# A two-block transformer kernel on one core: score banks, the place of a head's last mix, five more orders, and who splits one weight tile

## The chip, the cores and the metric

The kernel is one launch on one core of a Trainium2 chip. The metric is the device time in microseconds. TensorE (PE in the rows) multiplies; VectorE (DVE), ScalarE (ACT) and GpSimd (POOL) compute beside it; SyncE (SP) issues most loads. The granted clock is the share of TensorE's full clock of 2.4 GHz that it was given; 0.50 is its lower level, 1.2 GHz.

## The reference

All in float32, for 512 tokens of width 1024 and a context of 256 tokens.

```python
def reference(x, p, ...):
    x = first_block(x, p, ...)        # NSA and sliding-window attention, conv MLP, gate
    return second_block(x, c_2, ctx_2, ...)

def second_block(x, c, ctx, ...):     # layer 0: diff_attention_mixer, layer 1: gqa_mixer
    h  = rms_norm(x, pre_g[i]) * (1.0 + scale) + shift
    hc = rms_norm(xc, pre_g[i]) * (1.0 + cscale) + cshift
    # diff attention, 8 heads: keys and values of tokens and context together
    o1 = sweep_attention(q[..., 0, :], k[..., 0, :], v)
    o2 = sweep_attention(q[..., 1, :], k[..., 1, :], v)
    o = rms_norm(o1 - lam * o2, subln_g) * (1.0 - lam_init)
    y = (o * silu(z)) @ w_out
    x = x + gate * rms_norm(y, post_g[i])   # layer 0 also for the context
    # layer 1: rms_norm of q and k by head, rope, softmax attention, 2 key heads
```

## The kernel before

Each engine has its own instruction list, written out by hand, and semaphores ("signals") join them: `x.up(event)` counts, `wait_ge(x.at(event))` waits. The order of an engine's instructions is the order of its code, so an instruction that waits holds up all behind it.

**Products.** Float32 is kept by splitting each operand into a high and a low half: `three` (L482) issues three matmuls per chunk (L483 to L485): high by high and the two mixed products. Weights are loaded by SyncE in pairs of 128-row chunks into two raw buffers (`sp_program`, L371; a buffer is loaded again when its pair is split) and split by GpSimd (`pool_program`, L432: L470 makes the high half `w_hi`, L472 the low half `w_lo`, twice per pair). The tile ("kv", 1) is the second of all; then GpSimd zeroes keys.

**End of the first attention (project_out).** For each of four row tiles t: product with w_o, norm, addition; ScalarE squares (L1513) and scales the row (L1517), TensorE turns it (`turn_out`, L517), ScalarE writes h_hi (L1495), VectorE h_lo (L2311). `pe_first_cols` (L934) multiplies the first 256 tokens by the next weight in four units of eight chunks (24 matmuls) between the last turns.

**Gate stage.** Units u = 0 to 7 on VectorE; in u = 7 the sum of the last mod piece (`dve_mod_sum`, `dve_mod_end`, L2553), which TensorE turns at L894.

**Heads.** Eight heads of the difference attention. A head has six query tiles, `HEAD_TILES` = context tiles 4 and 5, then token tiles 0 to 3; n = 0 to 11 counts a tile's two halves. For each n: scores on TensorE (L1184; a context tile has 256 columns in bank 0, a token tile 2 × 384 in banks 0 and 1), the minimum on VectorE (L2797), the exponential with its sum on ScalarE (L2034). After both halves VectorE mixes them (`dve_head_mix`, L2805, L2807, L2809), TensorE turns the mix in two parts through one bank (L1200), ScalarE copies each part (L2045), and two tiles later come the values (L1214). The last tile's mix is done in the next head at n = 0, behind that head's first minimum. Between the scores TensorE works off, by `HEAD_FILL`, the chunks of the next head's projections ("beside": 4 chunks behind n = 0, 2 and 1 behind n = 1); their rows go through ScalarE (L1972, L1979, L1980) and VectorE (ropes L2743 to L2752, L2769, L2770) and TensorE (L1133).

**out0 and the last layer.** `pe_out0` multiplies by w_out and turns rows 0 to 5 (ScalarE: tmp L1505, h_hi L1509; VectorE: h_lo L2318), then the key rows kv8. `dve_keys8` (L2892) finds the roots of two key tiles (L2271 to L2287), scales by them (L2903) and ropes them; `dve_grouped` (L2985) begins with the query tables gq, q_cos, q_sin, L2990 to L2996; `dve_turned8` (L2919) gives k_lo, and TensorE turns keys at L1333.

## Time and profile before

| | us |
|---|---|
| median of 3 runs | 1715.09 (1714.62 to 1715.71) |
| the profiled execution, its own time | 1713.1 |
| its span | 1711.8 |
| its granted clock, mean | 0.966 |
| TensorE matmul busy | 1576.5 (92%) |
| VectorE busy | 1043.0 (61%) |
| GpSimd busy | 708.9 (41%) |
| ScalarE busy | 623.5 (36%) |
| TensorE's waits for L2034 before L1184, from 928 to 1290 us, 13 of them | 19.5 |

The time of a run is some 1.3 us longer than the span of the trace. A matmul's duration in a row overlaps the next one's; their starts show the pace. A number in square brackets at the end of a timeline row is the time for which the engine did nothing before it, and the arrow names the instruction whose end released it.

### The profile page before, as it was taken

Reading aid. Unit: us, or ns where it says so; the run is one execution under the profiler, and the core shown is the slowest. Engines: PE = TensorE matmul, PEld = TensorE weight load, DVE = VectorE, ACT = ScalarE, POOL = GpSimd, SP = SyncE. Lnnn points to the kernel's source line nnn. Section 1 sums busy time; section 2 is a strip of 40 time slices with the busy share of each in tenths; the row PEclk is TensorE's granted clock in tenths of the full one; section 3 lists DMA queues with packets and bytes.
Section 4 is the critical chain, followed back from the end, with each engine's and each line's share of the span. In section 5 each row is a group of like instructions: output and inputs, shape, how many; then the busy total and the mean of one; then the engine's idle time right before and its main releaser. Section 6 shows DMA issues by size and latency. Waiting matters only on the chain.

```text
span 1711.8 us, 21954 instructions
## 1 busy us (share of the span) xinstructions
PE 1576.5 (92%) x7933; PEld 1305.5 (76%) x7933; DVE 1043.0 (61%) x2136; ACT 623.5 (36%) x1506; POOL 708.9 (41%) x676
## 2 busy tenths in 40 slices
PE   5998799989999999999899999999997988899997
PEld 4786344788877887877788988898895777788886
DVE  7636665447777658658555665565566366665644
ACT  3213566231222210123633443444344356344431
POOL 6855000346776749667313303312334213333430
PEclk9997999989999999999999999999999999999999
DMA  6622000424444445553211001101112321110221
GB/s 181 196 72 87 1 1 1 136 82 141 131 125 133 135 157 178 175 168 123 84 28 50 27 24 50 50 13 38 50 38 62 133 77 50 50 50 25 74 87 50
DMA packets 115884, 142.58 MB, mean 83 GB/s; under 512 B 11048, under 2 KB 75200, under 8 KB 115776
## 3 DMA queue, kind: packets, MB, share of 16 engines
q1 hardware_dynamic: 89968, 91.77, 17.6%
q10 hardware_dynamic: 25808, 49.40, 8.9%
q8 instruction: 64, 1.05, 0.2%
q14 instruction: 44, 0.36, 0.1%
HBM read 132.74 MB, written 8.40 MB: 82 GB/s over the span
## 4 chain that ended last, share of the span: by engine, by line
PE 35%; DVE 9%; ACT 4%; issue 2%; ACTq 0%; DVEq 0%
PE ps L483 7%; PE ps L484 7%; PE ps L485 7%; PE ps L1214 3%; PE ps L1184 3%; PE ps L1407 2%; PE ps L1384 2%; PE ps L1200 2%; PE ps L1133 1%; PE ps L1396 1%; ACT tmp L1505 1%; DVE st L2797 1%; DVE newton L2281 1%; ACT p L2034 1%; DVE p L2809 1%
## 5 line engine op out<-in xcount | busy, mean ns | idle before, releaser
L470 POOL TENSOR_SCALAR w_hi<-w_raw 128x512 fp32r<-128x512 f32 x316 | 238.6, 755 | 718.7 <-PE ps L485 552.8
L472 POOL TENSOR_TENSOR w_lo<-w_raw,w_hi 128x512 fp32r<-128x512 f32 x316 | 438.6, 1388 | 26.4
L483 PE MATMUL ps<-w_hi,h_hi 128*128 128x384 f32 (+2 forms) x768 | 283.4, 369 | 3.0 <-DVE h_lo L2861 1.0
L484 PE MATMUL ps<-w_lo,h_hi 128*128 128x384 f32 (+2 forms) x768 | 269.1, 350 | 0.0
L485 PE MATMUL ps<-w_hi,h_lo 128*128 128x384 f32 (+2 forms) x768 | 268.6, 350 | 0.0
L483 PE MATMUL ps<-h_hi,w_hi 128*128 128x512 f32 (+1 forms) x616 | 245.9, 399 | 8.0 <-POOL w_lo L472 4.1
L484 PE MATMUL ps<-h_lo,w_hi 128*128 128x512 f32 (+1 forms) x616 | 238.5, 387 | 0.0
L485 PE MATMUL ps<-h_hi,w_lo 128*128 128x512 f32 (+1 forms) x616 | 238.4, 387 | 0.0
L2531 DVE SCALAR_TENSOR_TENSOR mod_acc<-mod_piece,csil,mod_acc 128x512 f32<-128x512 f32 x140 | 157.7, 1166 | 25.6 <-DMA mod_piece<-in_ada_w 21.2
L483 PEld LDWEIGHTS ps<-w_hi,h_hi 128*128 128x128 f32 x768 | 148.6, 194 | 14.6 <-issue 1.6
L484 PEld LDWEIGHTS ps<-w_lo,h_hi 128*128 128x128 f32 x768 | 148.6, 193 | 9.6 <-issue 0.5
L485 PEld LDWEIGHTS ps<-w_hi,h_lo 128*128 128x128 f32 x768 | 147.9, 193 | 10.3
L483 PEld LDWEIGHTS ps<-h_hi,w_hi 128*128 128x128 f32 x616 | 117.5, 191 | 32.1 <-POOL w_lo L472 5.0
L485 PEld LDWEIGHTS ps<-h_hi,w_lo 128*128 128x128 f32 x616 | 117.2, 190 | 25.8
L484 PEld LDWEIGHTS ps<-h_lo,w_hi 128*128 128x128 f32 x616 | 117.8, 191 | 22.3
L2034 ACT ACTIVATE p<-ps,st 128x768 f32<-128x768 f32 (+1 forms) x96 | 72.9, 759 | 114.6 <-DVE st L2797 114.6
L2797 DVE TENSOR_REDUCE st<-ps 128x1 f32<-128x768 f32 (+1 forms) x96 | 74.4, 775 | 64.3 <-PE ps L1184 64.3
L483 PE MATMUL ps<-w_hi,g_hi 128*128 128x512 f32 x240 | 98.0, 408 | 4.9 <-POOL w_lo L472 4.7
L485 PE MATMUL ps<-w_hi,g_lo 128*128 128x512 f32 x240 | 95.8, 399 | 0.0
L484 PE MATMUL ps<-w_lo,g_hi 128*128 128x512 f32 x240 | 95.8, 399 | 0.0
L2045 ACT COPY p_turned<-ps 128x512 f32<-128x512 f32 (+1 forms) x80 | 36.6, 457 | 115.5 <-PE ps L1200 115.4
L2769 DVE SCALAR_TENSOR_TENSOR q<-ps,q 64x256 fp32r<-64x256 f32 x48 | 20.5, 428 | 93.6 <-ACT k_hi L1980 93.1
(322 smaller groups left out, 2840.1 us busy)
## 6 DMA issues: line engine op xcount, KB each, us to landing
...
w_raw<-in_a_w_in SPq DMA_DIRECT2D x128, 128.0 KB, 2.3
w_raw<-in_w_down SPq DMA_DIRECT2D x22, 512.0 KB, 3.9
w_raw<-in_b_w_in SPq DMA_DIRECT2D x20, 512.0 KB, 3.7
w_raw<-in_w_out SPq DMA_DIRECT2D x16, 512.0 KB, 3.8
w_raw<-in_w_in SPq DMA_DIRECT2D x8, 512.0 KB, 4.0
w_raw<-in_w_o SPq DMA_DIRECT2D x8, 512.0 KB, 3.8
```

Source lines behind the costliest of these rows:

```text
L470: pool.tensor_scalar(hi[:, e, :], raw[:, e, :], 1.0, 0.0, ALU.mult, ALU.add).then_inc(*s["pool_step"].up())
L472: m = pool.tensor_tensor(lo[:, e, :], raw[:, e, :], hi[:, e, :], ALU.subtract)
L483: pe.matmul(out, a[0], b[0], start=start, stop=False)
L484: pe.matmul(out, a[0], b[1], start=False, stop=False)
L485: return pe.matmul(out, a[1], b[0], start=False, stop=stop)
L1184: m = pe.matmul(k.ps[:, j, 0:cols], k.q6[:, b, sub, t * P:(t + 1) * P], kk[:, b, sub, k0 + j * cols:k0 + (j + 1) * cols], start=first, sto ...
L1200: m = pe.transpose(k.ps[:, 4, a * P:(a + 1) * P], k.p6[:, i % 2, c0:c0 + P], k.ident[:, :])
L1214: m = pe.matmul(out, k.v6[:, hd % 2, c, :], k.at6[:, c, :], start=c == chunks[0], stop=c == TA - 1)
L2034: act.activation(folded(k.p6[:, i % 2 if sub == 0 else 2, 0:w], bs), bank_view(k, bs, P, cols), ACT.Exp, bias=f[:, sub:sub + 1], scale=-1. ...
L2045: act.copy(k.at6[:, chunks[0]:chunks[-1] + 1, (t % 2) * P:(t % 2 + 1) * P], k.ps[:, 4, 0:P * len(chunks)].rearrange("p (c n) -> p c n", n= ...
L2531: m = dve.scalar_tensor_tensor(acc, piece, w, acc, ALU.mult, ALU.add)
L2797: dve.tensor_reduce(k.st6[:, i % 4, sub:sub + 1], bank_view(k, bs, P, cols), AX.XY if len(bs) == 2 else AX.X, ALU.min).then_inc(*s["head_l ...
```

## The change

Seven places; what each does:

- Tile ("kv", 1): ScalarE writes the high halves, one activation of 128x1024 per pair, behind its early loads and ahead of its copies of the key halves; GpSimd writes only the low halves and waits for ScalarE's signal.
- project_out: TensorE turns row 2 behind the unit i = 1 (was 2) and row 3 behind six chunks of the unit i = 3 (was behind the whole); ScalarE squares row 3 before the h_hi of row 2 (was behind).
- Gate stage: the last mod piece's sum and end move on VectorE from u = 7 to u = 6, before a turn.
- Heads: context scores alternate between banks 0 and 1, and wait for the exponential two before, where the bank was last read.
- Heads: the last tile's mix stands behind its own head's last minimum (n = 11), not in the next head.
- out0: TensorE turns row 0 behind both halves of tile 3.
- out0 on VectorE: the query tables are made at t = 4 of the loop; the roots of the first keys stand before the last turn, with no wait for the table load.

```diff
@@ -416,6 +416,10 @@
+BY_SCALAR = ("kv", 1)
 def pool_zero_keys(k, pool):
@@ -465,10 +469,13 @@
                     pool.wait_ge(*s["roped8"].at(("kv8", TX + 1)))
+            if tile == BY_SCALAR:
+                pool.wait_ge(*s["act_step"].at(("w_hi", q)))
             for e in range(2):
-                pool.tensor_scalar(hi[:, e, :], raw[:, e, :], 1.0, 0.0, ALU.mult, ALU.add).then_inc(*s["pool_step"].up())
-                pool.wait_ge(*s["pool_step"].now())
+                if tile != BY_SCALAR:
+                    pool.tensor_scalar(hi[:, e, :], raw[:, e, :], 1.0, 0.0, ALU.mult, ALU.add).then_inc(*s["pool_step"].up())
+                    pool.wait_ge(*s["pool_step"].now())
                 m = pool.tensor_tensor(lo[:, e, :], raw[:, e, :], hi[:, e, :], ALU.subtract)
@@ -598,6 +605,20 @@
     return None
+def score_banks(n):
+    return ([0, 1], 384) if HEAD_TILES[n // 2] < TX else ([n % 2], C)
+def scores_before(hd, n):
+    if n == 2 * TC:
+        return (hd, n - 1)
+    if 2 <= n < 2 * TC:
+        return (hd, n - 2)
+    return (hd, n - 1) if n > 1 else (hd - 1, 11) if hd > 0 else None
@@ -920,10 +941,11 @@
     for i in range(4):
-        pe_first_cols(k, pe, i, 0)
-        if i == 2:
+        pe_first_cols(k, pe, i, 0, range(KD) if i < 3 else range(FIRST_TURN_AT))
+        if i == 1:
             turn_out(TX - 2)
     turn_out(TX - 1)
+    pe_first_cols(k, pe, 3, 0, range(FIRST_TURN_AT, KD))
@@ -931,10 +953,13 @@
-def pe_first_cols(k, pe, i, half):
+FIRST_TURN_AT = 6
+def pe_first_cols(k, pe, i, half, chunks=range(KD)):
     out, cols = k.ps[:, ff_bank(0, i), half * 256:half * 256 + 256], slice(half * 256, half * 256 + 256)
-    for c in range(KD):
+    for c in chunks:
         if c % 2 == 0:
@@ -1176,12 +1201,12 @@
     t = HEAD_TILES[i]
-    k0, cols, banks = (0, 384, 2) if t < TX else (S, C, 1)
-    if (hd, n) != (0, 0):
-        pe.wait_ge(*s["head_exped"].at((hd, n - 1) if n > 0 else (hd - 1, 11)))
+    k0, (banks, cols) = 0 if t < TX else S, score_banks(n)
+    if scores_before(hd, n) is not None:
+        pe.wait_ge(*s["head_exped"].at(scores_before(hd, n)))
     for first, kk in ((True, k.k6), (False, k.k6lo)):
-        for j in range(banks):
-            m = pe.matmul(k.ps[:, j, 0:cols], k.q6[:, b, sub, t * P:(t + 1) * P], kk[:, b, sub, k0 + j * cols:k0 + (j + 1) * cols],
+        for j, bank in enumerate(banks):
+            m = pe.matmul(k.ps[:, bank, 0:cols], k.q6[:, b, sub, t * P:(t + 1) * P], kk[:, b, sub, k0 + j * cols:k0 + (j + 1) * cols],
                           start=first, stop=not first)
@@ -1312,7 +1337,7 @@
                     pe_out0_chunk(k, pe, t, nh, c)
-            if t >= 3 and nh == 0:
+            if t >= 3 and nh == (1 if t == 3 else 0):
                 turn_out(t - 3)
@@ -1570,6 +1595,10 @@
         pass
+    for q in range(0, KD, 2):
+        pair = (KD + q) // 2
+        act.wait_ge(*s[f"w_loaded{pair % 2}"].at(pair))
+        act.activation(k.place(BY_SCALAR)[0][:, q:q + 2, :], k.w_raw[:, pair % 2, :, :], ACT.Copy, scale=1.0).then_inc(*s["act_step"].up(("w_hi", q)))
     for j in range(3):
@@ -1747,8 +1776,8 @@
         act.dma_start(k.x_dram[:, t, :], k.x2[:, t, :]).then_inc(*s["x_out"].up(("1", t), 16))
+    act_last_squares(k, act, "y1", TX - 1, k.x2, rows)
     turn_out(TX - 2)
-    act_last_squares(k, act, "y1", TX - 1, k.x2, rows)
     act_last_scale(k, act, "y1", TX - 1, k.x2, rows, "out1")
@@ -2020,7 +2049,7 @@
     t, f = HEAD_TILES[i], k.st6[:, i % 4, :]
-    bs, cols = ([0, 1], 384) if t < TX else ([0], C)
+    bs, cols = score_banks(n)
     w = cols * len(bs)
@@ -2696,8 +2725,6 @@
             dve_gate_y(k, dve, TX - 1)
-        if u == 7:
-            dve_mod_sum(k, dve, *LAST_MOD, 4)
         if u >= 5:
@@ -2708,14 +2735,15 @@
             dve_gate_turn_out(k, dve, TX + u - 2)
+        if u == 6:
+            dve_mod_sum(k, dve, *LAST_MOD, 4)
+            dve_mod_end(k, dve, 1)
         if u >= 6:
             dve_lambda(k, dve)
-        if u == 7:
-            dve_mod_end(k, dve, 1)
     dve_gate_rms(k, dve, TX - 1)
@@ -2792,7 +2820,7 @@
     i, sub = n // 2, n % 2
-    bs, cols = ([0, 1], 384) if HEAD_TILES[i] < TX else ([0], C)
+    bs, cols = score_banks(n)
     dve.wait_ge(*s["head_scored"].at((hd, n)))
@@ -2846,8 +2874,11 @@
             dve_head_least(k, dve, hd, n)
-            if n % 2 == 0 and (hd, n) != (0, 0):
-                dve_head_mix(k, dve, *((hd, n // 2 - 1) if n > 0 else (hd - 1, 5)))
+            if n % 2 == 0 and n > 0:
+                dve_head_mix(k, dve, hd, n // 2 - 1)
+            if n == 11:
+                dve_head_mix(k, dve, hd, 5)
             if n == 3 and hd > 0:
@@ -2861,7 +2892,6 @@
             pass
-    dve_head_mix(k, dve, 7, 5)
     dve_head_gate(k, dve, 7)
@@ -2879,22 +2909,44 @@
             turn_out(t - 3)
+        if t == TX:
+            dve_query_tables(k, dve)
         dve_add(k, dve, "y3", t, k.x7, k.y7[:, t % 2, :], OUT0_BANKS[t % 3], k.post7[:, t // TX, :], t > 0,
     turn_out(TA - 2)
+    dve_roots_of_keys8(k, dve, 0)
     turn_out(TA - 1)
+    dve_keys8(k, dve, 0)
+def dve_query_tables(k, dve):
+    s, half = k.sig, GD // 2
     dve.wait_ge(*s["tabb_in"].at("all"))
-    dve_keys8(k, dve, 0)
+    dve.wait_ge(*s["x_out"].at(("7", TX - 1)))
+    dve.wait_ge(*s["scaled"].at(("out3", 2)))
+    dve.tensor_scalar(k.gq[:, :], k.gq[:, :], GD ** -0.5, None, ALU.mult).then_inc(*s["gq_ready"].up("gq"))
+    dve.wait_ge(*s["gq_ready"].at("gq"))
...
+    dve.tensor_tensor(k.qsin[:, :, 0:half], k.sinb[:, :, 0:half], gains[:, :, half:GD].to_broadcast([P, TX, half]), ALU.mult)
...
+def dve_roots_of_keys8(k, dve, i):
+    dve.wait_ge(*k.sig["raw_sq"].at(("kv8", 2 * i + 1)))
+    dve_rsqrt(k, dve, k.ssk[:, 1, 4 * i:4 * i + 4], k.ssk[:, 0, 4 * i:4 * i + 4], GD, ("kv8", i))
     rstd = k.ssk[:, 1, 4 * i:4 * i + 4]
-    dve.wait_ge(*s["raw_sq"].at(("kv8", 2 * i + 1)))
-    dve_rsqrt(k, dve, rstd, k.ssk[:, 0, 4 * i:4 * i + 4], GD, ("kv8", i))
     dve.wait_ge(*s["rms"].at(("kv8", i)))
@@ -2984,25 +3036,16 @@
     s = k.sig
-    step = s["dve_step"]
-    half = GD // 2
-    dve.tensor_scalar(k.gq[:, :], k.gq[:, :], GD ** -0.5, None, ALU.mult).then_inc(*s["gq_ready"].up("gq"))
-    dve.wait_ge(*s["gq_ready"].at("gq"))
...
-    dve.tensor_tensor(k.qsin[:, :, 0:half], k.sinb[:, :, 0:half], gains[:, :, half:GD].to_broadcast([P, TX, half]), ALU.mult)
...
     def key_turned(t):
+    dve_roots_of_keys8(k, dve, 1)
     dve_keys8(k, dve, 1)
     key_turned(1)
+    dve_roots_of_keys8(k, dve, 2)
     dve_keys8(k, dve, 2)
```

VectorE around the end of a head (1051 is the minimum of n = 11, 1052 to 1058 low halves and ropes of the next head's rows). Before:

```order
1051 L2797 TENSOR_REDUCE st_155<-ps 128x1 [waits head_scored]
1052 L2769 SCALAR_TENSOR_TENSOR q_148<-ps,q_148 64x2x128 [waits head_hi]
1053 L2770 TENSOR_TENSOR k_lo<-ps,k_hi 128x2x128
1054 L2743 TENSOR_TENSOR rot_133<-ps,cos_a 128x4x64 [waits dve_step,head_turned,head_v]
1055 L2745 TENSOR_TENSOR rot6b<-ps,sin_a 128x4x32
1056 L2746 TENSOR_TENSOR rot6b<-ps,sin_a 128x4x32
1057 L2750 TENSOR_TENSOR rot_133<-rot_133,rot6b 128x4x64 [waits dve_step]
1058 L2752 TENSOR_TENSOR rot_133<-rot_133,rot6b 128x4x64 [waits dve_step]
1059 L2797 TENSOR_REDUCE st_155<-ps 128x1 [waits head_scored]
1060 L2805 RECIPROCAL st_155<-st_155 128x2 [waits head_exped]
1061 L2807 TENSOR_SCALAR p_129<-p_129,st_155,lam 128x768 [waits dve_step]
1062 L2809 SCALAR_TENSOR_TENSOR p_129<-p_129,st_155 128x768 [waits dve_step]
```

After:

```order
1051 L2825 TENSOR_REDUCE st_155<-ps 128x1 [waits head_scored]
1052 L2833 RECIPROCAL st_155<-st_155 128x2 [waits head_exped]
1053 L2835 TENSOR_SCALAR p_129<-p_129,st_155,lam 128x768 [waits dve_step]
1054 L2837 SCALAR_TENSOR_TENSOR p_129<-p_129,st_155 128x768 [waits dve_step]
1055 L2797 SCALAR_TENSOR_TENSOR q_148<-ps,q_148 64x2x128 [waits head_hi]
1056 L2798 TENSOR_TENSOR k_lo<-ps,k_hi 128x2x128
1057 L2771 TENSOR_TENSOR rot_133<-ps,cos_a 128x4x64 [waits dve_step,head_turned,head_v]
1058 L2773 TENSOR_TENSOR rot6b<-ps,sin_a 128x4x32
1059 L2774 TENSOR_TENSOR rot6b<-ps,sin_a 128x4x32
1060 L2778 TENSOR_TENSOR rot_133<-rot_133,rot6b 128x4x64 [waits dve_step]
1061 L2780 TENSOR_TENSOR rot_133<-rot_133,rot6b 128x4x64 [waits dve_step]
1062 L2825 TENSOR_REDUCE st_155<-ps 128x1 [waits head_scored] x2
```

The mix of three instructions has moved ahead of the low halves and ropes, and the first two minimums of the next head stand together.

ScalarE at the end of project_out (L1495 and L1520 are h_hi, L1513 and L1538 the squares, L1517 and L1542 the scale). Before:

```order
268 L1495 ACTIVATE h_hi<-ps,gx 128x128 [waits turn_ps]
269 L1495 ACTIVATE h_hi<-ps,gx 128x128 x3
270 L1495 ACTIVATE h_hi<-ps,gx 128x128 [waits turn_ps]
271 L1495 ACTIVATE h_hi<-ps,gx 128x128 x3
272 L1513 ACTIVATE rows_72,halves<-x_80 128x1024 [waits added]
273 L1517 ACTIVATE rows_72<-x_80,stat 128x1024 [waits rms]
274 L1495 ACTIVATE h_hi<-ps,gx 128x128 [waits turn_ps]
```

After:

```order
272 L1538 ACTIVATE rows_72,halves<-x_80 128x1024 [waits added]
273 L1520 ACTIVATE h_hi<-ps,gx 128x128 [waits turn_ps]
274 L1520 ACTIVATE h_hi<-ps,gx 128x128 x3
275 L1520 ACTIVATE h_hi<-ps,gx 128x128 [waits turn_ps]
276 L1520 ACTIVATE h_hi<-ps,gx 128x128 x3
277 L1542 ACTIVATE rows_72<-x_80,stat 128x1024 [waits rms]
278 L1520 ACTIVATE h_hi<-ps,gx 128x128 [waits turn_ps]
```

The squares have gone ahead of the four h_hi rows of row 2.

VectorE from the last turns of out0 to the second keys (L2318 and L2347 are h_lo, `ssk` the roots, `gq`, `q_cos`, `q_sin` the tables). Before:

```order
1606 L2318 TENSOR_TENSOR h_lo<-tmp_159,h_hi 128x4x128 [waits turn_hi] x4
1607 L2271 TENSOR_SCALAR ssk<-ssk 128x4 [waits rms,raw_sq,tabb_in]
1608 L2274 TENSOR_SCALAR newton<-ssk 128x4 [waits dve_step]
1629 L2749 TENSOR_TENSOR raw_160<-rotk,rotkb 128x256 [waits dve_step]
1630 L2990 TENSOR_SCALAR gq<-gq 128x128
1631 L2992 TENSOR_TENSOR q_cos<-cos_b,gq 128x512 [waits gq_ready]
1632 L2995 TENSOR_TENSOR q_sin<-sin_b,gq 128x4x64
1633 L2996 TENSOR_TENSOR q_sin<-sin_b,gq 128x4x64
1634 L2271 TENSOR_SCALAR ssk<-ssk 128x4 [waits rms,raw_sq]
```

After:

```order
1603 L2347 TENSOR_TENSOR h_lo<-tmp_159,h_hi 128x4x128 [waits turn_hi] x2
1604 L2300 TENSOR_SCALAR ssk<-ssk 128x4 [waits rms,raw_sq]
1605 L2303 TENSOR_SCALAR newton<-ssk 128x4 [waits dve_step]
1615 L2316 SCALAR_TENSOR_TENSOR ssk<-newton,ssk 128x4 [waits dve_step]
1616 L2347 TENSOR_TENSOR h_lo<-tmp_159,h_hi 128x4x128 [waits turn_hi] x2
1617 L2955 SCALAR_TENSOR_TENSOR raw_160<-raw_160,ssk,gk 128x128 [waits raw_in,rms]
1618 L2955 SCALAR_TENSOR_TENSOR raw_160<-raw_160,ssk,gk 128x128
```

The roots stand between the last two turns, and the tables are no longer here; they stand some 50 rows earlier.

## Rows read from the trace of the kernel before

**Rows 1.** Timeline of TensorE at two head boundaries: start, us, what, [idle before].

```profile
983.27 0.28 PE L1184 MATMUL ps<-k_hi,q 128*128 128x256 f32 x1
...
988.06 0.39 PE L1184 MATMUL ps<-k_hi,q 128*128 128x256 f32 x1 [2.29 <-ACT p L2034]
...
989.30 1.12 PE L1200 MATMUL ps<-ident,p 128*128 128x128 f32 x4 [0.74 <-DVE p L2809]
...
993.21 0.36 PE L1184 MATMUL ps<-k_hi,q 128*128 128x256 f32 x1
...
1042.25 0.28 PE L1184 MATMUL ps<-k_hi,q 128*128 128x256 f32 x1
...
1053.21 0.50 PE L1184 MATMUL ps<-k_hi,q 128*128 128x256 f32 x1
```

**Rows 2.** Timeline of VectorE, in and after a head's last tile.

```profile
973.33 0.95 DVE L2807 TENSOR_SCALAR p<-p,st,lam 128x768 f32<-128x768 f32 x1
974.31 1.25 DVE L2809 SCALAR_TENSOR_TENSOR p<-p,st 128x768 f32<-128x768 f32 x1
...
983.62 0.43 DVE L2769 SCALAR_TENSOR_TENSOR q<-ps,q 64x256 fp32r<-64x256 f32 x1 [3.97 <-ACT k_hi L1980]
...
985.70 1.37 DVE L2752 TENSOR_TENSOR rot<-rot,rot6b 128x256 f32<-128x256 f32 x1
...
988.23 1.02 DVE L2809 SCALAR_TENSOR_TENSOR p<-p,st 128x768 f32<-128x768 f32 x1
```

**Rows 3.** Timeline of ScalarE at the same boundary.

```profile
979.68 0.90 ACT L2034 ACTIVATE p<-ps,st 128x768 f32<-128x768 f32 x1
...
987.44 0.47 ACT L2034 ACTIVATE p<-ps,st 128x256 f32<-128x256 f32 x1 [3.70 <-DVE st L2797]
...
990.46 0.58 ACT L2045 COPY p_turned<-ps 128x512 f32<-128x512 f32 x1 [2.45 <-PE ps L1200]
```

**Rows 4.** Window 980 to 996: busy by engine, granted clock, DMA share, GB/s.

```profile
980.00:996.00 16.00, 12.96 (x72) 11.98 (x71) 7.55 (x18) 5.04 (x16) 6.54 (x7) 0.89 0.35 99
```

**Rows 5.** Second weight tile: GpSimd, TensorE, ScalarE, then its loads.

```profile
56.32 0.62 POOL L470 TENSOR_SCALAR w_hi<-w_raw 128x512 fp32r<-128x512 f32 x1
57.02 1.26 POOL L472 TENSOR_TENSOR w_lo<-w_raw,w_hi 128x512 fp32r<-128x512 f32 x1
...
58.33 0.50 PE L483 MATMUL ps<-h_hi,w_hi 128*128 128x512 f32 x1 [2.22 <-POOL w_lo L472]
...
49.11 0.59 ACT L1578 ACTIVATE k_hi_twice<-ps 64x512 fp32r<-64x512 f32 x1 [25.18 <-PE ps L485]
...
w_raw<-in_w_in SPq DMA_DIRECT2D x2, 512.0 KB, 3.7
```

**Rows 6.** End of project_out: TensorE, ScalarE, and the window's clock.

```profile
365.38 1.97 PE L517 MATMUL ps<-ident,rows 128*128 128x128 f32 x8 [3.49 <-ACT rows L1517]
369.92 0.58 PE L483 MATMUL ps<-h_hi,w_first_hi 128*128 128x256 f32 x1 [2.57 <-DVE h_lo L2311]
...
358.63 2.17 ACT L1495 ACTIVATE h_hi<-ps,gx 128x128 fp32r<-128x128 f32 x8 [4.39 <-PE ps L517]
...
364.18 1.15 ACT L1517 ACTIVATE rows<-x,stat 128x1024 f32<-128x1024 f32 x1 [2.34 <-DVE stat L2287]
...
364.00:374.00 10.00, 6.05 (x27) 5.65 (x28) 2.30 (x9) 3.32 (x9) 9.13 (x10) 0.50 0.28 72
```

**Rows 7.** Keys of the last layer: VectorE, then TensorE.

```profile
1437.07 1.26 DVE L2271 TENSOR_SCALAR ssk<-ssk 128x4 f32<-128x4 f32 x1
...
1449.53 0.42 DVE L2996 TENSOR_TENSOR q_sin<-sin_b,gq 128x256 f32<-128x256 f32 x1
...
1456.91 1.09 PE L1333 MATMUL ps<-ident,raw 128*128 128x128 f32 x4 [4.89 <-DVE k_lo L2919]
```

**Rows 8.** TensorE in the gate stage and in out0.

```profile
841.62 0.37 PE L894 MATMUL ps<-ident,mod 128*8 128x128 f32 x1 [5.59 <-DVE mod L2553]
...
1377.84 1.54 PE L517 MATMUL ps<-ident,rows 128*128 128x128 f32 x6 [5.42 <-ACT rows L1517]
```

8 lines of the change are left out of this document (4 added, 4 removed).

## The prediction

> **What bounds the kernel now.** I read the page first. TensorE is busy for 92% of the span (table of the profile before), so time comes back only where its idle time, or the half-speed stretch behind an idle time, ends earlier. Next I read the waits of TensorE, to see which it meets again and again: between 928 and 1290 us it waits 13 times, 19.5 us in all, for the exponential L2034 before a head's scores (same table). Then the timelines of TensorE, VectorE and ScalarE around one head boundary, where each wait can be followed back to its start.
>
> **Two banks for context scores, last mix early (heads).** At 983.27 the first context score of a head is issued; the second, at 988.06, has waited 2.29 us for the exponential of the first, because both use bank 0; the transposes at 989.30 have waited 0.74 us for the mix of the head before; the third score follows at 993.21 [rows 1]. From first to third are 9.94 us. The reason is VectorE's order: it stood idle for 3.97 us until 983.62, then took the ropes (L2752 needs 1.37 us there), then the first minimum, then the mix, whose last step ends at 989.25 [rows 2]. ScalarE's exponential, 987.44 to 988.0, follows that minimum, and its copy of the transposes costs 0.58 us [rows 3].
>
> After the change the mix can start when the last exponential ends, 979.68 + 0.90 + the accumulator read, about 980.7 [rows 3], inside the idle 3.97 us. GpSimd is then splitting weights. Under such splitting another mix took 0.95 + 1.25 us [rows 2]; with the reciprocal (0.15) and issue it ends near 983.2, 0.4 us before VectorE's next input, so ropes, minimum and exponential stay where they were. TensorE's new timetable: score 983.27, its 12 products to 985.6 (0.175 us each from start to start), second score without waiting to 985.9, four transposes to 986.3, six products to 987.4. Then a new wait: the next two transposes use the same bank as the four, and ScalarE copies it only behind its exponential, 988.0 + 0.6, so until about 988.65, 1.2 us. Two transposes, three products and four transposes (1.25 us) end at 989.9, where the third score stands. That is 6.6 us instead of 9.94: 3.3 us less.
>
> The granted clock reads 0.89 in the 16 us around this boundary [rows 4]: behind the long gap the products go at half speed. With 1.2 us of idle instead of 3.0 I take them at full speed, which is in the 3.3. Two boundaries lie longer at half (as the one at 1042.25 needs 10.96 us to its third score [rows 1]), so 4.35 each. Two more are as at 983, the first (its gap is longer, 2.66 us) gives 3.6, the last, where products of 512 columns stand between, 2.5 by the same timetable. In head 0 only the second score's own wait goes, 1.5. Sum over seven boundaries and head 0: 3.6 + 3 × 3.3 + 2 × 4.35 + 2.5 + 1.5 = 26.2. Ends: if the clock stays at half wherever it is now, only idle comes back, 2.29 + 0.74 − 1.2 = 1.85 × 7 + 1.5 = 14.5; if the copy wait is half as long and nothing drifts, 31.
>
> Here a rule of the Trainium skill speaks against the new place. The row shows the last step of a mix at 1.25 us beside GpSimd's splits, 1.02 where they had ended [rows 2]. The skill ("SBUF — State Buffer", section "SBUF: two separate sides") says that a VectorE operation with two SBUF inputs and a GpSimd operation that reads SBUF lock each other out for a whole instruction, whichever starts first. By the row the mix grows by a quarter, by a full lock-out it could end a further 1 us later, at 984.2, and shift each boundary by 0.6, 4 us in all. The 1.37 us of L2752 [rows 2], beside a split, look like such a wait; I still go by the row of the mix itself.
>
> **Second weight tile.** TensorE waits 1.87 and 2.22 us for the third and fourth pair of this tile; the last is issued at 58.33 when GpSimd's split ends [rows 5]. GpSimd pays 0.62 + 1.28 us twice per pair; without the high halves 2.6 instead of 3.9. ScalarE is idle there for 25.18 us until 49.11 [rows 5], and a 128x1024 activation costs it 1.15 [rows 6]. But a raw buffer is loaded again only after its split, and that load takes 3.7 us [rows 5]: load 3.7, high 1.15, low 2.6 give a turn of 7.5 for two pairs, and the last pair is ready at about 56.15: 2.1 less. Ends 1.0 (ScalarE starts late) and 3.0. ScalarE's eight copies of key halves move from 49.1 to about 53.5; their reader on GpSimd comes later still, so this costs nothing; if that cover were gone it would be the shift minus this gain, some 2 us.
>
> **End of project_out.** TensorE waits 3.49 us for the last rows at 365.38 (ScalarE's scale 364.18 + 1.15), then 2.57 us for the low halves at 369.92, and the clock reads 0.50 from 364 to 374 [rows 6]. The rows behind it hang on the squares, which ScalarE does after the eight h_hi at 358.63. With turn_out(2) one unit (24 products, about 2.9 us) earlier, and the squares ahead of its h_hi, the h_hi start behind the squares at about 357.0, 1.6 earlier, and VectorE's root and the scale with them: last rows at 363.8. Six products held back fill part of the 2.57 us: 0.6 more. Sum 2.2; ends 1.2 (only part is passed on) and 4.5 (the half-speed stretch goes too: 10 us at 0.50 hold 5 us of lost work, of which I take half).
>
> **Gate stage and out0 turn.** The transposes at 841.62 waited 5.59 us for the sum of the last mod piece [rows 8]. VectorE now does it a step earlier, so this gap shrinks; but the next turn waits for ScalarE, which is busy without a break from 844.07 to 855.4 and starts by an input that the sum did not delay. TensorE arrives early and waits there: 0, at worst +1 (a step of the gate delayed on VectorE). At 1377.84 TensorE waited 5.42 us for rows of ScalarE [rows 8]; now it runs eight chunks first and waits later for the same chain, which goes through ScalarE and VectorE alone: 0, ends −0.5 and +0.5.
>
> **Query tables and roots.** From 1437.07 VectorE does 12 root steps on keys, several of them over 1.1 us long, 7.5 us in all, because they start only after both h_lo; the chain of waits runs through them, the ropes, the query tables (1448.33 to 1449.95, 1.6 us) and the second keys to TensorE, idle 4.89 us until 1456.91 [rows 7]. The tables go into an idle stretch of VectorE about 1405 (about +0.15 if they push h_lo). The roots' input is ready at about 1431.8; started there they end at 1439.4, the two h_lo follow to 1441, and keys(0) end at 1445 to 1447 instead of 1448.4. So 1.6 + 2.8 − 0.1 = 4.3. Ends 2.9 (roots gain only 1.3) and 6 (the half-speed products behind this gap). The late h_lo are due to TensorE only at its last key rows, about 1442: cover of 1 us.
>
> **Sum.** 26.2 + 2.1 + 2.2 + 4.3 + 0 = 34.8. The profiled execution took 1713.1 us (span 1711.8), so it would be 1678.3; it lies 2.0 below the median of the runs, 1715.09, so I predict 1680.3.
>
> **The rivals.** (a) Every gap that shrinks counts: the 5.59 and 5.42 us come back too, 11.0 more: 1669.3. For it: they are the longest of these gaps. Against: ScalarE without a break behind the one, the chain without TensorE behind the other. (b) The boundary keeps its half speed and gives 14.5 instead of 26.2: 1692.0. For it: the new wait of 1.2 us lies just where the clock is low now. Against: it is less than half of the idle time that stands before the half-speed products now. The lock-out of the Trainium skill's page would give 1684.3, inside the forecast's own range. (c) The slower side: the mix stands ahead of the q and k_lo steps and the ropes in VectorE's queue; if it ends after 983.6, all of them, the first minimum, exponential and copy move one for one, and TensorE's products wait for the banks that the ropes free. At 3.3 us per boundary (mix ending about 987) the gain is gone; at 6 it is a loss of 2.7 × 7 = 19, and with 34.8 − 26.2 = 8.6 gained by the rest the time is 1715.1 + 19 − 8.6 = 1725.5. Against: it would need a mix of 8.9 us (980.7 to 989.6) where the slowest row shows 2.4. (d) The change does nothing that is measured: the copy wait is as long as the two waits that it replaces (3.0 us), and the other gains end in later waits, as in the gate stage: 1713 to 1717.
>
> **How the numbers follow.** Forecast (1674 to 1688) 0.62; (a) 0.12; (b) 0.20; (c) 0.03; (d) 0.03. The range takes in (a) and (b) and the ends of the parts: 1668 to 1693. About 0.2% is what a measurement of this kernel can tell from no change, here 3.4 us. Faster 0.94, same 0.03, slower 0.03.
>
> **What would show it.** Heads: second score right behind the products, mix inside VectorE's idle before the q step, new wait at the two transposes of about 1.2 us, first to third score 6.6 us, clock 1.00. Second tile: last wait for w_lo under 0.5 us. project_out: last rows near 363.8. Gate and out0: the two gaps gone, the same time in later waits for tmp. Keys: wait before 1456.91 shorter by four. Wrong if: the mix ends after the q step could start, the clock stays low, or the ropes grow.

## The result and the profile after

The changed kernel takes 1673.89 us (median of 4 runs, 1671.12 to 1675.06); the kernel before, run beside it, 1714.86. The ratio is 0.9765, with a 95% interval of 0.9742 to 0.9789, so about 40 us less; predicted were 34.8 less, with 1668 to 1693 us as the range. In the profiled executions the span fell from 1711.8 to 1673.1 us, 38.7 less. The page of the kernel after, busy time of TensorE and its granted clock in 40 slices:

```profile
PE 1564.0 (93%) x7933; PEld 1294.8 (77%) x7933; DVE 1048.0 (63%) x2136; ACT 626.9 (37%) x1510; POOL 708.5 (42%) x668
...
PEclk8998999999999999999999999999998999999999
```

Single executions of one kernel differ by 4 us and more; in the two traces of the changed kernel, 2.9 us of difference are stretches at half speed that one has and the other has not. Small parts are therefore read from the traces stage by stage: the same TensorE instruction is found in both traces, and the difference of its start times is followed from stage to stage. A stage's number is how much that difference changes within the stage; a minus is time gained. The kernel after against the kernel before, from trace to trace, and, where an experiment undoes the part, what it gives back in its stage:

| stage (position in the trace before) | predicted | measured | given back when undone |
|---|---|---|---|
| second weight tile (to 75 us) | −2.1 | −2.1 | 1.8 in its two waits |
| end of project_out (345 to 376) | −2.2 | −3.3 | 2.9 |
| gate stage (780 to 870) | 0 | +0.3 | 0 |
| head 0, second score (870 to 882) | −1.5 | −1.7 | 1.7 (one bank) |
| seven head boundaries (882 to 1303) | −24.7 | −29.9 | 17.2 (one bank), 35.3 (late mix) |
| out0 and keys (1303 to 1490) | −4.3 | −1.1 | roots 1.1, tables 1.5 at the keys |
| everything else | 0 | −0.9 | |

**The boundary.** TensorE at the boundary that answers to [rows 1] (score L1209, transposes L1225), then VectorE (last step of the mix L2837, last rope step L2780), GpSimd and ScalarE:

```profile
970.64 0.28 PE L1209 MATMUL ps<-k_hi,q 128*128 128x256 f32 x1
...
972.97 0.28 PE L1209 MATMUL ps<-k_hi,q 128*128 128x256 f32 x1
...
973.21 0.60 PE L1225 MATMUL ps<-ident,p 128*128 128x128 f32 x4
...
975.46 0.44 PE L1225 MATMUL ps<-ident,p 128*128 128x128 f32 x2 [0.59 <-ACT p_turned L2074]
...
976.62 0.36 PE L1209 MATMUL ps<-k_hi,q 128*128 128x256 f32 x1
```

```profile
969.19 1.92 DVE L2837 SCALAR_TENSOR_TENSOR p<-p,st 128x768 f32<-128x768 f32 x1
...
973.28 0.72 DVE L2780 TENSOR_TENSOR rot<-rot,rot6b 128x256 f32<-128x256 f32 x1
```

```profile
968.83 1.46 POOL L479 TENSOR_TENSOR w_lo<-w_raw,w_hi 128x512 fp32r<-128x512 f32 x1
...
972.94 0.79 POOL L477 TENSOR_SCALAR w_hi<-w_raw 128x512 fp32r<-128x512 f32 x1
```

```profile
974.37 0.47 ACT L2063 ACTIVATE p<-ps,st 128x256 f32<-128x256 f32 x1 [3.26 <-DVE st L2825]
...
974.83 0.57 ACT L2074 COPY p_turned<-ps 128x512 f32<-128x512 f32 x1
```

The second score (972.97) follows the products without a wait, and the transposes (973.21) follow it. The two waits of [rows 1] have become one of 0.59 us, at 975.46, for ScalarE's copy behind its exponential (974.83). First to third score are 5.98 us (970.64 to 976.62). They were 9.94 here and 9.94 to 10.96 over the seven. Six boundaries now read 5.98 to 6.01, the last 7.13. The half speed of [rows 4] is gone: the window 963 to 979 is at full clock, and so is TensorE at all seven boundaries, where the kernel before spent 27.3 us at half speed. TensorE's idle time in the seven intervals fell from 20.3 to 3.6 us.

```profile
963.00:979.00 16.00, 15.41 (x93) 14.46 (x92) 10.72 (x23) 5.43 (x16) 11.54 (x11) 1.00 0.43 123
```

**The other stages.** End of project_out, TensorE (last rows, first product behind them) and the window 356 to 376, for [rows 6]:

```profile
361.76 1.96 PE L524 MATMUL ps<-ident,rows 128*128 128x128 f32 x8 [2.77 <-ACT rows L1542]
...
366.30 0.39 PE L490 MATMUL ps<-h_hi,w_first_hi 128*128 128x256 f32 x1 [1.29 <-DVE h_lo L2340]
...
356.00:376.00 20.00, 15.94 (x120) 15.44 (x120) 9.70 (x33) 7.04 (x19) 14.62 (x16) 0.91 0.27 82
```

The last rows wait 2.77 us (3.49 before), the next product 1.29 (2.57), and the half-speed stretch is about 20 × 0.09 × 2 = 3.6 us long instead of 10. The last rows stand 1.4 us earlier against the work before them. From them to the next product are 4.54 us, as before (369.92 − 365.38). Second weight tile, for [rows 5], waits of the third and fourth pair:

```profile
53.67 0.50 PE L490 MATMUL ps<-h_hi,w_hi 128*128 128x512 f32 x1 [0.66 <-POOL w_lo L479]
...
56.69 0.50 PE L490 MATMUL ps<-h_hi,w_hi 128*128 128x512 f32 x1 [1.36 <-POOL w_lo L479]
```

They were 1.87 and 2.22, so the two gained 2.1. Gate stage and out0, for [rows 8]:

```profile
831.51 0.63 PE L524 MATMUL ps<-ident,y 128*128 128x128 f32 x4 [1.99 <-ACT tmp L1530]
833.48 1.11 PE L524 MATMUL ps<-ident,y 128*128 128x128 f32 x4 [1.33 <-ACT tmp L1530]
...
840.80 0.63 PE L524 MATMUL ps<-ident,y 128*128 128x128 f32 x4 [1.22 <-ACT tmp L1530]
842.77 0.86 PE L524 MATMUL ps<-ident,y 128*128 128x128 f32 x4 [1.33 <-ACT tmp L1530]
...
1350.71 0.63 PE L524 MATMUL ps<-ident,rows 128*128 128x128 f32 x4 [3.77 <-ACT tmp L1530]
1352.67 1.11 PE L524 MATMUL ps<-ident,rows 128*128 128x128 f32 x4 [1.34 <-ACT tmp L1530]
```

The 5.59 us wait is gone and four waits for ScalarE's tmp have come, 1.99 + 1.33 + 1.22 + 1.33 = 5.87; the 5.42 us in out0 has turned into 3.77 + 1.34 = 5.11. Keys, for [rows 7]: VectorE (first root step, scaling L2955, rope L2771), TensorE's wait, and the window 1440 to 1444:

```profile
1393.54 0.48 DVE L2300 TENSOR_SCALAR ssk<-ssk 128x4 f32<-128x4 f32 x1 [1.99 <-ACT junk_k L2194]
...
1402.81 2.00 DVE L2955 SCALAR_TENSOR_TENSOR raw<-raw,ssk,gk 128x128 f32<-128x128 f32 x2
1404.84 1.49 DVE L2771 TENSOR_TENSOR rotk<-raw,cos_b 128x256 f32<-128x256 f32 x1
...
1416.01 0.63 PE L1358 MATMUL ps<-ident,raw 128*128 128x128 f32 x4 [3.36 <-DVE k_lo L2971]
...
1440.00:1444.00 4.00, 3.96 (x17) 3.86 (x18) 1.96 (x4) 1.07 (x2) 0.00 (x0) 0.57 0.00 0
```

The roots start at 1393.54, but the scaling of the first keys takes 2.00 us and its rope 1.49. TensorE's wait is 3.36 us instead of 4.89, but the clock reads 0.57 from 1440 to 1444; at that place, 39 to 41 us later in its own trace, the kernel before was at full clock.

### The profile page after: what moved, and what is told of

Its sections match the earlier page's. It is cut to its first block and busy times, and to the rows that moved or that the text cites. A ratio compares the mean times of both kernels' runs of the same rounds, so it can differ in the third digit from the quotient of the medians.

```text
span 1673.1 us, 21955 instructions
## 1 busy us (share of the span) xinstructions
PE 1564.0 (93%) x7933; PEld 1294.8 (77%) x7933; DVE 1048.0 (63%) x2136; ACT 626.9 (37%) x1510; POOL 708.5 (42%) x668
## 5 line engine op out<-in xcount | busy, mean ns | idle before, releaser
L479 POOL TENSOR_TENSOR w_lo<-w_raw,w_hi 128x512 fp32r<-128x512 f32 x316 | 438.2, 1387 | 31.0 <-ACT w_hi L1601 5.3
L2560 DVE SCALAR_TENSOR_TENSOR mod_acc<-mod_piece,csil,mod_acc 128x512 f32<-128x512 f32 x140 | 156.0, 1154 | 24.7 <-DMA mod_piece<-in_ada_w 20.6
L876 PE MATMUL ps<-pt,v 128*64 128x512 f32 x108 | 59.2, 643 | 14.3 <-ACT pt L1693 14.0
```

What stands on the lines that cost most here:

```text
L479: m = pool.tensor_tensor(lo[:, e, :], raw[:, e, :], hi[:, e, :], ALU.subtract)
L876: m = pe.matmul(out, k.v[:, c, v0:v0 + HD], k.pt1[:, n % 3, :], start=first, stop=last)
L2560: m = dve.scalar_tensor_tensor(acc, piece, w, acc, ALU.mult, ALU.add)
```

## The experiments

All kernels start from the changed one, and each short diff is against it; three dots mark lines left out. Every run had the kernel before beside it on its chip: 1713.49 us for the first four, 1714.04 for the next four, 1711.37 for the last four.

**The changed kernel once more.** 

> The changed kernel once more, as the reference for the kernels beside it on the same chip, and to see which stretches of half speed come back in another execution at the same place. All theories: 1674, stages with the same waits as in the first trace; the six waits of 0.59 us at a head boundary are there again.

1671.55 us (5 runs, 1670.99 to 1677.33), ratio 0.9753 (0.9728 to 0.9778). The heads' stages agree with the first trace within 0.1 us each. The profiled run was 2.9 us longer in span. All of it comes from two places where nothing was changed: a half-speed stretch at 515 us that was 6.8 us long instead of 3.4, and one of 3.4 us at 566 that the first trace lacks, for 1.5 us each. That is the measure of luck in a total.

**Late mix, two banks.**

```diff
-            if n % 2 == 0 and n > 0:
-                dve_head_mix(k, dve, hd, n // 2 - 1)
-            if n == 11:
-                dve_head_mix(k, dve, hd, 5)
+            if n % 2 == 0 and (hd, n) != (0, 0):
+                dve_head_mix(k, dve, *((hd, n // 2 - 1) if n > 0 else (hd - 1, 5)))
...
+    dve_head_mix(k, dve, 7, 5)
```

> The changed kernel with one part undone: the last mix of a head stands again in the next head, behind its first minimum; the context scores keep their two banks. Theory (the two parts need each other, because VectorE's order sets the boundary): the second score goes early into bank 1, but the transposes behind it wait some 3.3 us for the mix, and first to third score is again about 9.5 to 10 us instead of 5.98. Of the 31.6 us that the heads gained, head 0's 1.7 stays and little else: about 28 us more than the changed kernel, 1702 (1697 to 1706). Rival (each part carries its own share of the gain): the banks alone keep about half, 1688 to 1692.

1703.07 us (7 runs, 1701.96 to 1710.92), ratio 0.9949 (0.9930 to 0.9968). TensorE at a boundary, and the window around it:

```profile
978.47 0.28 PE L1209 MATMUL ps<-k_hi,q 128*128 128x256 f32 x1
...
980.80 0.28 PE L1209 MATMUL ps<-k_hi,q 128*128 128x256 f32 x1
...
984.50 1.04 PE L1225 MATMUL ps<-ident,p 128*128 128x128 f32 x4 [3.31 <-DVE p L2837]
...
988.73 0.36 PE L1209 MATMUL ps<-k_hi,q 128*128 128x256 f32 x1
```

```profile
976.00:992.00 16.00, 12.69 (x69) 12.02 (x68) 7.97 (x18) 4.37 (x14) 5.74 (x6) 0.89 0.30 87
```

The second score goes early (980.80), the transposes then wait 3.31 us for the mix, and first to third are 10.26 us: worse than the 9.94 before the change. Over the seven boundaries the trace loses 35.3 us against the changed kernel, more than the two parts together had gained there (29.9). The theory holds: banks without the early mix cost 5.3 us there. In the seven intervals TensorE's idle time is 23.4 us where it was 20.3 before the change, and the half-speed stretches are 37.5 us long together where they were 27.3. One of the seven mixes is a test by itself, since it meets a split that the others miss:

```profile
1103.07 1.90 DVE L2837 SCALAR_TENSOR_TENSOR p<-p,st 128x768 f32<-128x768 f32 x1
```

GpSimd's w_lo had begun at 1102.48 there and ended at 1104.16; the other six mixes had no split beside them and took 1.02 us in this step. The wait of the transposes at this boundary is the longest of the seven, 4.20 us.

**Early mix, one bank.**

```diff
-    return ([0, 1], 384) if HEAD_TILES[n // 2] < TX else ([n % 2], C)
+    return ([0, 1], 384) if HEAD_TILES[n // 2] < TX else ([0], C)
...
-    if n == 2 * TC:
-        return (hd, n - 1)
-    if 2 <= n < 2 * TC:
-        return (hd, n - 2)
-    return (hd, n - 1) if n > 1 else (hd - 1, 11) if hd > 0 else None
+    return (hd, n - 1) if n > 0 else (hd - 1, 11) if hd > 0 else None
```

> The changed kernel with one part undone: all context scores again in bank 0, so that the second waits for the exponential of the first; the mix stays early. Theory: the second score waits about 2.0 us at each of seven boundaries, then the transposes and the copy follow without a wait; first to third score about 7.3 us at full clock (5.98 now), up to 8.5 if the wait brings the half-speed stretch back; head 0 loses 1.7. So 9 + 1.7 = 11 to 19 us more: 1685 to 1693, most likely 1688. Rival (the banks alone make the gain): 1700 and more.

1693.44 us (4 runs), ratio 0.9879 (0.9863 to 0.9895). TensorE at a boundary and its window:

```profile
974.25 0.28 PE L1205 MATMUL ps<-k_hi,q 128*128 128x256 f32 x1
...
978.63 0.39 PE L1205 MATMUL ps<-k_hi,q 128*128 128x256 f32 x1 [1.89 <-ACT p L2059]
...
983.14 0.36 PE L1205 MATMUL ps<-k_hi,q 128*128 128x256 f32 x1
...
972.00:988.00 16.00, 14.11 (x77) 13.32 (x76) 8.41 (x17) 5.03 (x16) 6.52 (x6) 0.89 0.29 84
```

A wait of 1.89 us is left, 8.89 us from first to third, and the clock reads 0.89 as before the change. The total lies at the upper end of the theory, where the half speed comes back, and not at its likeliest 1688. The first boundary has the same wait of 1.89 us and no half-speed stretch behind it; it takes 7.34 us. Five others have a stretch of 3.4 us and take 8.84 to 8.89. So at a boundary the longer wait costs 1.4 us (7.34 − 5.98) and the stretch 1.5 more.

The early mix alone gains 12.7 us, banks alone lose 3.6 net of head 0's 1.7, and together they gain 31.6. Each part alone leaves a wait of 1.8 us or more at six boundaries (1.2 or more at the last), most often with a half-speed stretch behind it. With both, the wait is 0.59 to 0.66 us (1.0 at two boundaries of 48), and no stretch at half speed stands at a boundary in any of the eight profiled executions with this order of the heads.

**Roots behind the last h_lo.**

```diff
-    dve_roots_of_keys8(k, dve, 0)
     turn_out(TA - 1)
+    dve_roots_of_keys8(k, dve, 0)
```

> The changed kernel with one part undone: the roots of the first two key tiles stand again behind both last h_lo. Theory (the roots' early start was spent again, because the scaling and ropes of the keys then ran beside GpSimd's splits): the first keys end about 1.1 us later than now, TensorE's wait for k_lo is 1.1 longer, 1675.0. Rival 1 (my prediction's term): 2.8 us later, 1676.7. Rival 2 (the extra half-speed stretch at 1416 to 1420 comes from the pattern of waits that the early roots made): it vanishes and the kernel is within 0.5 us of 1673.9 or below.

1677.37 us (4 runs, 1673.9 to 1680.1; the profiled run has a span of 1672.6), ratio 0.9786 (0.9766 to 0.9806). VectorE (first root step, first scaling), TensorE's wait and the window 1440 to 1444:

```profile
1399.33 1.25 DVE L2300 TENSOR_SCALAR ssk<-ssk 128x4 f32<-128x4 f32 x1
...
1406.88 0.61 DVE L2955 SCALAR_TENSOR_TENSOR raw<-raw,ssk,gk 128x128 f32<-128x128 f32 x2
...
1417.64 1.09 PE L1358 MATMUL ps<-ident,raw 128*128 128x128 f32 x4 [3.36 <-DVE k_lo L2971]
...
1440.00:1444.00 4.00, 2.58 (x19) 2.55 (x20) 2.17 (x6) 1.67 (x3) 0.00 (x0) 1.00 0.10 39
```

The wait for k_lo ends 1.1 us later than in the changed kernel (in the stage times), as the theory said, and not 2.8. The median is no help in this: 1677.37 is nearer to rival 1's 1676.7. Behind the wait 1.8 us came back: the changed kernel's half-speed stretch between 1441 and 1444 us is not there. It was in both profiled executions of the changed kernel and in two others (early mix with one bank, and the last kernel below), not in the other nine; what brings it is open. It is not the stretch at 1416 us that the expectation names, since the kernel before has that one too, at 1456. In total this kernel is not told apart from the changed one by its trace; its median is 3.5 us above that of the first measurement, with ratio intervals that overlap.

**Query tables between the keys.**

```diff
-        if t == TX:
-            dve_query_tables(k, dve)
...
+    dve.wait_ge(*k.sig["tabb_in"].at("all"))
     dve_keys8(k, dve, 0)
...
+    dve_query_tables(k, dve)
     dve_roots_of_keys8(k, dve, 1)
```

> The changed kernel with one part undone: the query tables are made again between the first and the second keys; the roots stay early. Theory (the tables were on the chain): the wait for k_lo before 1416 us is 1.6 us longer and stays so to the end, apart from stretches at half speed. Rival: VectorE has slack there, under 0.3 us.

1673.94 us (4 runs), ratio 0.9788 (0.9773 to 0.9802). The wait in question:

```profile
1416.22 1.09 PE L1358 MATMUL ps<-ident,raw 128*128 128x128 f32 x4 [4.89 <-DVE k_lo L2970]
```

4.89 us instead of 3.36: the tables were on the chain, and their 1.5 us is real. Counted from 1441 us of the trace before, this kernel is 1.6 us behind the changed one at 1466. At 1490 the two are level, because the changed kernel's execution has the extra half-speed stretch and this one hasn't.

**Gate stage and out0 as before.**

```diff
+        if u == 7:
+            dve_mod_sum(k, dve, *LAST_MOD, 4)
...
-        if u == 6:
-            dve_mod_sum(k, dve, *LAST_MOD, 4)
-            dve_mod_end(k, dve, 1)
...
+        if u == 7:
+            dve_mod_end(k, dve, 1)
```

> The changed kernel with one part undone: the last mod piece is summed again in the last unit of the gate stage. Theory: the wait of 5.6 us before its transposes is back and nothing behind it is later, since the change had moved the heads by +0.3 us against the gate stage's start: 1673.6. Rival (each gap counts): 1679.

```diff
-            if t >= 3 and nh == (1 if t == 3 else 0):
+            if t >= 3 and nh == 0:
```

> The changed kernel with one part undone: in out0 TensorE turns row 0 again between the two halves of tile 3. Theory (off the path: the chain of ScalarE and VectorE sets the end of out0): the 5.42 us wait before those transposes is back, and the work behind is within 0.5 us: 1674.3. Rival (the longer gap costs what it says, and the clock behind it): 1677 to 1680.

The first gave 1672.66 us (ratio 0.9758, 0.9733 to 0.9783) and the second 1671.64 us (0.9750, 0.9727 to 0.9773), 5 runs each. TensorE in the first, then in the second:

```profile
834.02 0.38 PE L915 MATMUL ps<-ident,mod 128*8 128x128 f32 x1 [5.63 <-DVE mod L2582]
...
1338.61 1.97 PE L524 MATMUL ps<-ident,rows 128*128 128x128 f32 x8 [5.09 <-ACT rows L1542]
```

Both long waits are back, and neither costs anything: the gate stage takes 0.1 us more than before the change where the changed kernel took 0.3, within the spread of the other executions (0.0 to 0.7, and 1.9 in one, the kernel with the old project_out, which has a half-speed stretch there), and between 1303 and 1448 us the two orders of out0 differ by 0.1 us. In each place some five microseconds of idle time moved, and the work behind them came no earlier.

**End of project_out as before.**

```diff
-        pe_first_cols(k, pe, i, 0, range(KD) if i < 3 else range(FIRST_TURN_AT))
-        if i == 1:
+        pe_first_cols(k, pe, i, 0)
+        if i == 2:
             turn_out(TX - 2)
     turn_out(TX - 1)
-    pe_first_cols(k, pe, 3, 0, range(FIRST_TURN_AT, KD))
...
+    turn_out(TX - 2)
     act_last_squares(k, act, "y1", TX - 1, k.x2, rows)
-    turn_out(TX - 2)
```

> The changed kernel with one part undone: the end of project_out in its old order on TensorE and ScalarE. Theory: last rows 1.4 us later, the 2.57 us wait unfilled, and the stretch at half speed 10 us long again instead of 4: 3.3 us more within the trace from 350 to 380 us. Rival (the clock stretch is the luck of an execution and not of the order): 1.7 us more.

1677.81 us (4 runs), ratio 0.9809 (0.9792 to 0.9825). TensorE, its window 356 to 376, and the same window of the late-mix kernel, which has the new order here:

```profile
361.16 1.09 PE L524 MATMUL ps<-ident,rows 128*128 128x128 f32 x8 [3.49 <-ACT rows L1541]
365.24 0.58 PE L490 MATMUL ps<-h_hi,w_first_hi 128*128 128x256 f32 x1 [2.99 <-DVE h_lo L2339]
...
356.00:376.00 20.00, 13.52 (x96) 13.09 (x96) 9.07 (x32) 6.90 (x17) 14.98 (x17) 0.83 0.28 81
...
356.00:376.00 20.00, 15.92 (x102) 15.43 (x101) 8.40 (x31) 5.57 (x14) 15.51 (x17) 0.74 0.28 81
```

The stage takes 2.9 us more: 1.4 for the order, the rest clock (0.83 instead of 0.91). The products held back behind the rows have no part in it: from the last rows to the next product this kernel, without them, takes 4.08 us (361.16 to 365.24). That is less than the 4.54 of the changed kernel, whose transposes ran at half speed there. But the new order is no guard of the clock: the late-mix kernel read 0.74 in one execution and was 2.1 us slower there. So of the 3.3 us, 1.4 are shown to be the order's, and the clock's share differs between executions, though eleven of the twelve profiled executions with the new order show the 3.3 or more. Both late ones lost another 1.5 us at 470 to 480 us, by a stretch at half speed, and had it back by 526: they lack the one that the kernel before has at 521.

**GpSimd splits the second tile.**

```diff
-BY_SCALAR = ("kv", 1)
+BY_SCALAR = None
...
-    for q in range(0, KD, 2):
-        pair = (KD + q) // 2
-        act.wait_ge(*s[f"w_loaded{pair % 2}"].at(pair))
-        act.activation(k.place(BY_SCALAR)[0][:, q:q + 2, :], k.w_raw[:, pair % 2, :, :], ACT.Copy, scale=1.0).then_inc(*s["act_step"].up(("w_hi", q)))
```

> The changed kernel with one part undone: GpSimd makes the high halves of the second weight tile again. Theory: the last two waits for w_lo (1.87 and 2.22 us) are back; 1.6 us more at 75 us into the trace, 2.2 at 200 us. Rival (the load of the raw buffers is the bound either way): under 0.5 us more.

1675.57 us (4 runs), ratio 0.9793 (0.9778 to 0.9807).

```profile
54.48 0.50 PE L490 MATMUL ps<-h_hi,w_hi 128*128 128x512 f32 x1 [1.62 <-POOL w_lo L479]
...
58.37 0.50 PE L490 MATMUL ps<-h_hi,w_hi 128*128 128x512 f32 x1 [2.22 <-POOL w_lo L479]
```

The waits are back at 1.62 and 2.22 us, 0.66 and 1.36 with ScalarE's help, together 1.8 us. The theory holds for the waits in this pair of traces, and the load is not the only bound. The size is less sure than it looks: over the stage (40 to 75 us) this kernel gains 0.2 us on the kernel before. Ten of the twelve executions with ScalarE's help gain 1.4 to 3.0, and the other two (one bank, and late roots) only 0.5 and 0.6. What of it is left further on can't be told: at 345 us, counted from 40, this kernel stands at −2.6 us against the kernel before, and the executions with ScalarE's help at −1.7 to −5.2, by stretches at half speed between 75 and 345 us that came in some and not in others.

**A better order: ScalarE copies first.**

```diff
-            if late is not None:
+            if n == 0 and hd > 0:
+                act_head_at(k, act, hd - 1, 5, 0)
+            if late is not None and n > 1:
                 act_head_at(k, act, *late, 0)
             act_head_exp(k, act, hd, n)
```

> The changed kernel with one order more: ScalarE copies the first four transposes of the last mix before the next head's first exponential instead of behind it. Theory (the new wait of 0.59 us at the fifth transpose is ScalarE's order alone): six waits of 0.59 us go, the exponential starts at most 0.1 us later: 3.5 us less, 1670.4. Rival (the following work is bound by VectorE's minimum and the exponential anyway): the waits move to the third score, within 0.5 us of 1673.9.

1671.90 us (4 runs), ratio 0.9751 (0.9730 to 0.9773). TensorE (first score, fifth transpose, the product behind it, third score):

```profile
972.12 0.28 PE L1209 MATMUL ps<-k_hi,q 128*128 128x256 f32 x1
...
976.19 0.38 PE L1225 MATMUL ps<-ident,p 128*128 128x128 f32 x2
976.74 0.44 PE L490 MATMUL ps<-w_hi,h_hi 128*128 128x384 f32 x1 [0.17 <-POOL w_lo L479]
...
977.72 0.36 PE L1209 MATMUL ps<-k_hi,q 128*128 128x256 f32 x1
```

The wait of 0.59 us is gone and first to third are 5.60 us: 0.38 less at each of six boundaries, 2.3 us over the heads, where 3.5 were expected. Most of the rest went to a wait that lay behind it: the product after the fifth transpose now arrives before GpSimd's split of its weights (976.74, L479).

**One chunk moved.** Both tries keep ScalarE's copy first. The first put the chunk in the wrong place:

```diff
-HEAD_FILL = (4, (2, 1), 6, (5,), 6, (5,), 6, (3, 2), 6, (3, 2), 6, (3, 2))
+HEAD_FILL = (4, (2, 1), 6, (6,), 5, (5,), 6, (3, 2), 6, (3, 2), 6, (3, 2))
```

> The changed kernel with two orders more: ScalarE's copy ahead of the exponential as in the run before, and one chunk of the next head's projection moved from behind the fifth score of a head to behind the fourth (fill 6 and 5 instead of 5 and 6), on all engines. Theory: the fifth score of each head waits 0.63 us for the exponential of the fourth, seven times in this trace; one chunk (0.5 us) ahead of it fills most of that: 0.5 x 7 = 3.5 us less, beside 2.25 from the copy: 1668. Rival: a later fifth score only moves the wait to the sixth, and the fill gains nothing: 1671.5.

1668.93 us (5 runs, ratio 0.9734, 0.9707 to 0.9762); the wait of 0.63 us stayed, because it stands before the tenth score, not the fifth. The heads gained nothing beside the copy's 2.3 us. That the median met the expected 1668 is luck, as the term that was to bring 3.5 of it brought nothing. The second try:

```diff
-HEAD_FILL = (4, (2, 1), 6, (5,), 6, (5,), 6, (3, 2), 6, (3, 2), 6, (3, 2))
+HEAD_FILL = (4, (2, 1), 6, (5,), 6, (5,), 6, (3, 2), 7, (2, 2), 6, (3, 2))
```

> The changed kernel with the copy ahead of the exponential and one chunk of the next head's projection moved from behind the tenth score to behind the ninth (fill 7 and 2 + 2 instead of 6 and 3 + 2). The trace of the run before showed that the wait of 0.63 us stands before the tenth score (for the ninth's exponential), not before the fifth. Theory: a chunk of 256 columns (0.36 us) fills part of it: 0.36 x 7 = 2.5 us less than with the copy alone, about 4.7 less than the changed kernel. Rival: the minimum of the ninth stands behind the z step on VectorE, which comes later too: nothing gained.

1668.03 us (4 runs), ratio 0.9752 (0.9737 to 0.9766). The wait in this kernel, and in the changed one:

```profile
956.18 0.62 PE L1209 MATMUL ps<-k_hi,q 128*128 128x384 f32 x2 [0.28 <-ACT p L2063]
...
954.89 0.62 PE L1209 MATMUL ps<-k_hi,q 128*128 128x384 f32 x2 [0.63 <-ACT p L2063]
```

0.28 us instead of 0.63, and the heads are 5.0 us shorter than in the changed kernel (36.6 instead of 31.6 against before). By its ratio it isn't told apart from the changed kernel (0.9753 in the second measurement); by its trace it is the faster of the two in the stage that was edited. The rival, that nothing would be gained, falls with that.

## Why the prediction was right, and where it was off

**The total.** 1673.89 us is inside the range of 1668 to 1693 and just under the 1674 to 1688 that was held most likely. In the traces 38.7 us went where 34.8 were forecast. The parts missed by more than that, and their errors in part cancelled: the heads gave 5.4 more and project_out 1.1 more, the keys 3.2 less, and stages without an edit gave 0.9.

**Heads: mechanism right, 5.4 us too small.** The second score without a wait, the mix in VectorE's idle time but for its last 0.2 us, the one new wait at the fifth transpose and the clock at 1.00 came as forecast. The term that was mis-sized is the new wait: 1.2 us by the timetable, 0.59 measured, so first to third is 5.98 and not 6.6. The timetable kept the ropes as they were. They were not: their last step fell from 1.37 to 0.72 us (at all seven boundaries alike), so the first minimum and the exponential came some 0.45 us earlier against the first score, and the end of the copy 0.6 us before the timetable's. The first boundary was sized by its gap alone (3.6); its interval had been 10.61, and it gave 4.6.

**Where the ropes' time went.** The rows show VectorE's steps with two SBUF operands ending with GpSimd's instructions. Before, the rope step of [rows 2] ended at 987.07, 0.28 us behind GpSimd's, which ended at 986.8; now it ends at 974.00, 0.27 behind GpSimd's 972.94 + 0.79 = 973.73. The mix's last step took 1.92 us, from 969.19 to 971.11, while GpSimd's w_lo ran from 968.83 to 970.29; without GpSimd such a step takes 1.02. It is the same at all seven boundaries: in both traces of the changed kernel the mix ends 0.81 or 0.82 us behind GpSimd's instruction, and there and in the kernel before the last rope step ends 0.27 or 0.28 behind.

The row of 1.25 us in [rows 2] was no milder case. GpSimd's instruction beside it was nearer to its end:

```profile
973.83 0.93 POOL L470 TENSOR_SCALAR w_hi<-w_raw 128x512 fp32r<-128x512 f32 x1
```

It ended at 974.76, and the mix 0.80 us behind it, at 975.56. So 1.25 was not a price that could be carried to another place. This is the rule of the Trainium skill ("SBUF — State Buffer", section "SBUF: two separate sides") that I had weighed and set aside for that row. The trace agrees with the page: such a VectorE step outlasts GpSimd's instruction by a fixed time, and how long it takes follows from when that instruction ends. The prediction gave a full lock-out a mix that ends 1.0 us later than by the row. It ended 0.47 us behind the first score (971.11 against 970.64), where the row had put it 0.07 ahead of it (983.2 against 983.27), so 0.5 later. What the prediction did not see is that the later mix puts everything behind it at another place against GpSimd's splits. There the mix took 0.67 us more than the row, and the last rope step 0.65 less than before.

**Keys: 4.3 predicted, 2.7 at the first wait, 1.1 in the end.** The tables' 1.6 us was right (1.5 by the experiment). The roots' 2.8 was the step that failed: they started at 1393.54 as forecast and took 7.7 us, but scaling and ropes of the first keys, 3.8 us before, now ran beside GpSimd's last splits and took 6.2 (2.00 and 1.49 us for steps of 0.61 and 0.42). They ended at the late end of the 1445 to 1447 that the prediction gave them, and that left 1.1. The wait became 1.5 us shorter and not four. A half-speed stretch that the kernel before did not have at that place took 1.8 more in both executions of the changed kernel.

**project_out: 2.2 predicted, 3.3 measured.** The order gave 1.4 (1.6 predicted). The 0.6 for the six products held back came to nothing: TensorE waited for the rows on one side of them and for the low halves on the other, and both waits end on other engines' work. The rest, 1.9, came with the shorter half-speed stretch, for which the range had the end of 4.5; that the order shortens it is likely by the count of executions above, and not shown.

**Second tile, gate stage, out0's turn.** −2.1, 0 and 0 came out, the last two for the reasons given (+0.3 and 0.0 measured). For the second tile the sign named, a last wait under 0.5 us, did not appear: it was 1.36, because the gain was spread over two waits; and in two other executions the stage gained only 0.5 or 0.6. In the gate stage and out0 the waits for ScalarE took the place of the two long gaps almost to the microsecond. Rival (a), which counted these gaps, gave 1669.3 and would have been nearer to the total; its mechanism is refuted by both experiments. Rival (b) (half speed stays) did not occur here, but each head part alone brings it: 37.5 and 17.1 us at half speed over the seven boundaries, where it was 27.3. Rival (c) did not occur: the mix ended 0.2 us behind the point where the q step could have started, and that cost nothing.
